# One expert-weight stream per block: second blocks of an expert moved behind all first blocks

## The reference, cut to what matters

```
logits = hf @ router_w + router_b                    # 256 tokens x 32 experts
top_val, top_idx = lax.top_k(logits, TOP_K)          # TOP_K = 4
top_w = softmax(top_val)
...                                                  # tokens are grouped by expert
def expert_block(xb, e):
    g = xb @ w_gate[e] + b_gate[e]                   # 1024 x 1024
    u = xb @ w_up[e] + b_up[e]                       # 1024 x 1024
    g = minimum(g, 7); u = clip(u, -7, 7)
    act = g * sigmoid(1.702 * g) * (u + 1)
    return act @ w_down[e] + b_down[e]               # 1024 x 1024
y[token] += row_weight * expert_block(...)           # summed over a token's 4 experts
```

## Time and profile before

| | us |
|---|---|
| median of three runs | 2422.86 |
| the profiled execution | 2423.9 |
| its span, first to last instruction | 2422.1 |
| PE busy | 2315.6 |
| DVE busy | 1048.4 |
| ACT busy | 691.4 |

### The profile page before, as it was taken

One profiled execution on the slowest core, in us unless ns is written; L12 is line 12 of the kernel. 1 busy time (PEld: TensorE's weight loads), 2 busy tenths in 40 slices (PEclk: granted clock), 3 DMA queues, 4 the chain that ended last, 5 costly groups with the idle time before them and its releaser, 6 DMA issues.

```text
span 2422.1 us, 34200 instructions
## 1 busy us (share of the span) xinstructions
PE 2315.6 (96%) x13529; PEld 1558.5 (64%) x13530; DVE 1048.4 (43%) x1491; ACT 691.4 (29%) x945; POOL 4.9 (0%) x6
## 2 busy tenths in 40 slices
PE   6999899999999999999997999979999999999999
PEld 4667733333333333333335999969989899999998
DVE  7665241111111111111115765556565655576654
ACT  2122221110101001111005353354443544454443
POOL 0000000000000000000000000000000000000000
PEclk8999999999999999999998999989999999999999
DMA  9366379979999999799996555535555245544552
GB/s 367 115 226 253 133 291 422 422 320 422 422 422 422 422 422 421 331 422 422 422 422 237 187 201 180 187 126 200 184 189 182 95 176 190 185 174 172 191 184 94
DMA packets 93888, 657.03 MB, mean 271 GB/s; under 512 B 10308, under 2 KB 13144, under 8 KB 14840
## 3 DMA queue, kind: packets, MB, share of 16 engines
q1 hardware_dynamic: 91104, 648.19, 67.9%
q10 hardware_dynamic: 2712, 7.82, 1.0%
HBM read 654.84 MB, written 1.13 MB: 271 GB/s over the span
## 4 chain that ended last, share of the span: by engine, by line
PE 78%; DMA 16%; DVE 2%; ACT 2%; issue 1%; SPq 1%; ACTq 0%; DVEq 0%
PE psum L841 14%; DMA ring<-in_w_exp 13%; PE psum L525 13%; PE psum L524 13%; PE psum L526 13%; PE psum L865 6%; PE psum L592 3%; PE psum L693 2%; PE psum L818 2%; PE psum L875 2%; PE psum L731 1%; DMA ring<-in_w_ada 1%; DVE arena L1683 1%; PE psum L855 1%; DMA ring<-in_w_ffn 1%
## 5 line engine op out<-in xcount | busy, mean ns | idle before, releaser
L427 DVE TENSOR_TENSOR ring_parts<-ring,ring_parts 128x2048 fp32r<-128x2048 f32 x181 | 414.2, 2291 | 302.3 <-ACT ring_parts L1446 297.6
L524 PE MATMUL psum<-x_parts,ring_parts 128*128 128x256 f32 x1920 | 540.0, 281 | 3.6 <-DVE arena_parts L1683 3.6
L525 PE MATMUL psum<-arena_parts,ring_parts 128*128 128x256 f32 x1920 | 541.7, 282 | 0.0
L526 PE MATMUL psum<-x_parts,ring_parts 128*128 128x256 f32 x1920 | 538.0, 280 | 0.0
L841 PE MATMUL psum<-ring,arena 128*64 128x512 f32 x2176 | 484.8, 596 | 22.5 <-DMA ring<-in_w_exp 22.5
L524 PEld LDWEIGHTS psum<-x_parts,ring_parts 128*128 128x128 f32 x1920 | 362.5, 189 | 7.0 <-issue 5.4
L1446 ACT ACTIVATE ring_parts<-ring 128x2048 fp32r<-128x2048 f32 x181 | 342.3, 1906 | 83.9 <-DMA ring<-in_w_mix 54.3
L526 PEld LDWEIGHTS psum<-x_parts,ring_parts 128*128 128x128 f32 x1920 | 363.3, 189 | 0.0
L525 PEld LDWEIGHTS psum<-arena_parts,ring_parts 128*128 128x128 f32 x1920 | 361.9, 188 | 1.7
L841 PEld LDWEIGHTS psum<-ring,arena 128*64 128x64 f32 x2176 | 154.3, 137 | 310.8 <-issue 310.8
L1680 DVE TENSOR_SCALAR arena<-psum 128x512 f32<-128x512 f32 x68 | 47.0, 692 | 626.7 <-ACT arena L1424 450.9
(11 more groups left out here) (270 smaller groups left out, 1944.6 us busy)
## 6 DMA issues: line engine op xcount, KB each, us to landing
ring<-in_w_exp SPq DMA_DIRECT2D x384, 1024.0 KB, 18.0
ring<-in_w_ffn SPq DMA_DIRECT2D x132, 1024.0 KB, 4.8
ring<-in_w_mix SPq DMA_DIRECT2D x49, 1024.0 KB, 4.8
ring<-in_w_ada SPq DMA_DIRECT2D x24, 1024.0 KB, 6.4
ring<-in_w_in SPq DMA_DIRECT2D x16, 1024.0 KB, 9.8
arena<-gain_scratch ACTq DMA_DIRECT2D x10, 512.0 KB, 3.5
ring<-in_w_out SPq DMA_DIRECT2D x4, 1024.0 KB, 4.8
ring<-in_w_attn SPq DMA_DIRECT2D x2, 1024.0 KB, 4.8
```

The costliest lines, as they stand in the source:

```text
L427: return engine.tensor_tensor(ring_parts[:, s, :], ring[:, s, :], ring_parts[:, RAW + s, :], ALU.subtract)
L524: mm(out, w[0], a[0], start=start, stop=False, **more)
L525: mm(out, w[0], a[1], start=False, stop=False, **more)
L526: return mm(out, w[1], a[0], start=False, stop=stop, **more)
```

## The change

SP no longer follows the block list by expert. It fetches the experts 1 to 31 for the blocks 1 to 31, one block each, and then, if there are more than 32 blocks, fetches for every further block all 12 pieces of its expert, taken from `etab`. The block list becomes: first block of expert 0, of expert 1, ..., of expert 31, and then the second and later blocks of those experts that have them. `extra` now counts only the blocks beyond the first. Since block b always has its own 12 arrivals, PE waits by the block's number b, and its register load of `etab` in each turn of the loop goes. The tables are made on 16 x 32 elements in place of 49 x 32, by more instructions, and `starts` and the first of the two `tables` signals are gone.

```diff
@@ block.sync @@
-            sp.wait_ge(sem("tables"), 1)
-            with sp.Fori(1, E) as e:
-                first = sp.value_load(starts[0:1, bass.ds(e, 1)], min_val=1, max_val=BLOCKS)
-                for n in range(EXPERT_PIECES):
-
-                    sp.wait_ge(pieces, first * EXPERT_PIECES + (N_PRE + n + 1 - EXPERT_PIECES))
-                    sp.dma_start(ring[:, n, :], row("w_exp", e * EXPERT_PIECES + EXPERT_ORDER[n])).then_inc(full[n], 16)
-
-            sp.wait_ge(sem("tables"), 2)
+            with sp.Fori(1, E) as e:
+                for n in range(EXPERT_PIECES):
+
+                    sp.wait_ge(pieces, e * EXPERT_PIECES + (N_PRE + n + 1 - EXPERT_PIECES))
+                    sp.dma_start(ring[:, n, :], row("w_exp", e * EXPERT_PIECES + EXPERT_ORDER[n])).then_inc(full[n], 16)
+
+            sp.wait_ge(sem("tables"), 1)
             blocks = sp.value_load(nblk[0:1, 0:1], min_val=E, max_val=E + EXTRA)
+            with sp.If(blocks > E):
+                with sp.Fori(E, blocks) as b:
+                    e = sp.value_load(etab[0:1, bass.ds(b, 1)], min_val=0, max_val=E - 1)
+                    for n in range(EXPERT_PIECES):
+                        sp.wait_ge(pieces, b * EXPERT_PIECES + (N_PRE + n + 1 - EXPERT_PIECES))
+                        sp.dma_start(ring[:, n, :], row("w_exp", e * EXPERT_PIECES + EXPERT_ORDER[n])).then_inc(full[n], 16)
@@ block.tensor @@
-            def expert_weights(n, expert):
-                pe.wait_ge(full[n], expert * 16 + 16 * (fills_before[n] + 1))
+            def expert_weights(n, b):
+                pe.wait_ge(full[n], b * 16 + 16 * (fills_before[n] + 1))
...
-            pe.wait_ge(sem("tables"), 2)
+            pe.wait_ge(sem("tables"), 1)
             blocks = pe.value_load(nblk[0:1, 0:1], min_val=E, max_val=E + EXTRA)
             with pe.Fori(1, blocks) as b:
-                expert = pe.value_load(etab[0:1, bass.ds(b, 1)], min_val=0, max_val=E - 1)
...
-                hidden(0, expert)
-                hidden(1, expert)
+                hidden(0, b)
+                hidden(1, b)
...
-                down(b, expert)
+                down(b)
@@ DVE, the tables @@
-            step(ts(extra, cnt, float(CAP), 1.0, ALU.is_gt, ALU.add))
+            step(ts(extra, cnt, float(CAP), None, ALU.is_gt))
...
-            v.tensor_copy(starts[:], start).then_inc(sem("tables"), 1)
-            step(tt(ended, across(co("block"), E), along(end_, BLOCKS), ALU.is_ge))
-            step(v.tensor_reduce(owner, ended, AX_X, ALU.add))
-            step(tt(ended, ended, along(extra, BLOCKS), ALU.mult))
-            step(v.tensor_reduce(ahead, ended, AX_X, ALU.add))
-            step(tt(ahead, co("block"), ahead, ALU.subtract))
-            ts(basetab[:], ahead, float(CAP), None, ALU.mult)
-            ts(etab[:], owner, float(E - 1), None, ALU.min)
-            ts(nblk[:], end_[:, E - 1:E], 0.0, None, ALU.add).then_inc(sem("tables"), 1)
+            step(tt(cmp_a, across(co("extra"), E), along(start, EXTRA), ALU.is_ge))
+            step(tt(cmp_b, across(co("extra"), E), along(end_, EXTRA), ALU.is_lt))
+            step(tt(picked, cmp_a, cmp_b, ALU.mult))
+            step(tt(cmp_a, picked, along(co("expert"), EXTRA), ALU.mult))
+            step(v.tensor_reduce(xe, cmp_a, AX_X, ALU.add))
+            step(tt(cmp_b, across(co("extra"), E), along(start, EXTRA), ALU.subtract))
+            step(ts(cmp_b, cmp_b, 1.0, float(CAP), ALU.add, ALU.mult))
+            step(tt(cmp_b, cmp_b, picked, ALU.mult))
+            step(v.tensor_reduce(xb, cmp_b, AX_X, ALU.add))
+            v.memset(etab[:], 0)
+            step(v.memset(basetab[:], 0.0))
+            v.tensor_copy(etab[:, 0:E], co("expert"))
+            v.tensor_copy(etab[:, E:E + EXTRA], xe)
+            v.tensor_copy(basetab[:, E:E + EXTRA], xb)
+            ts(nblk[:], end_[:, E - 1:E], float(E), None, ALU.add).then_inc(sem("tables"), 1)
```

More of the change, by code:

```diff
@@ L83 @@
 for _name, _w in (("ident", P), ("ones", P), ("before", P), ("rotate", P), ("causal", P), ("flip", P),
-                  ("inv_freq", 1), ("eps", 1), ("slot", CAP), ("slot_of_row", 1), ("block", BLOCKS),
+                  ("inv_freq", 1), ("eps", 1), ("slot", CAP), ("slot_of_row", 1), ("extra", EXTRA), ("expert", E),
                   ("bucket", 2 * T - 1), ("one_hot", E), ("group_sum", 1)):
@@ L135, in constants @@
     put("slot_of_row", (i % CAP)[:, None])
-    put("block", np.tile(np.arange(BLOCKS), (P, 1)))
+    put("extra", np.tile(np.arange(EXTRA), (P, 1)))
+    put("expert", np.tile(np.arange(E), (P, 1)))
     b = t5_bucket(np.arange(-(T - 1), T))
@@ L283, in build @@
         basetab = sb("basetab", [P, BLOCKS])
-        starts = sb("starts", [P, E], I32)
         nblk = sb("nblk", [P, 1], I32)
@@ L374, in build @@
         cnt, extra, start, end_, exc = (view(16664 + n * E, E) for n in range(5))
-        owner = view(16824, BLOCKS)
-        ahead = view(16824 + BLOCKS, BLOCKS)
-        ended = view(13312, BLOCKS, E)
+        xe = view(16824, EXTRA)
+        xb = view(16824 + EXTRA, EXTRA)
+        cmp_a = view(13312, EXTRA, E)
+        cmp_b = view(13312 + EXTRA * E, EXTRA, E)
+        picked = view(13312 + 2 * EXTRA * E, EXTRA, E)
         ada_parts = (ada_sum[:], diagonal[:].rearrange("p a i -> p (a i)"))
@@ L827, in turn_gathered, with hidden @@
                 last.then_inc(sem("g_turned"), 1)
-            def expert_weights(n, expert):
-                pe.wait_ge(full[n], expert * 16 + 16 * (fills_before[n] + 1))
+            def expert_weights(n, b):
+                pe.wait_ge(full[n], b * 16 + 16 * (fills_before[n] + 1))
                 return ring[:, n, :]
-            def hidden(which, expert):
+            def hidden(which, b):
                 bank, at_ = 4 + which, 4 * which
@@ L837, in hidden @@
                 for n in range(2):
-                    w = [expert_weights(at_ + 2 * n + half, expert) for half in range(2)]
+                    w = [expert_weights(at_ + 2 * n + half, b) for half in range(2)]
                     for k in range(4):
@@ L855, in spread, with down @@
                 mm(psum[:, 4, :], picked_e[0:E, :], posw[0:E, :], start=True, stop=True).then_inc(sem("spread_done"), 1)
-            def down(b, expert):
+            def down(b):
                 pe.wait_ge(sem("act_t_ready"), b + 1)
                 for n in range(4):
-                    w = expert_weights(DOWN_AT + n, expert)
+                    w = expert_weights(DOWN_AT + n, b)
                     for k in range(2):
@@ L913, in _ @@
             spread(0)
-            down(0, 0)
-            pe.wait_ge(sem("tables"), 2)
+            down(0)
+            pe.wait_ge(sem("tables"), 1)
             blocks = pe.value_load(nblk[0:1, 0:1], min_val=E, max_val=E + EXTRA)
             with pe.Fori(1, blocks) as b:
-                expert = pe.value_load(etab[0:1, bass.ds(b, 1)], min_val=0, max_val=E - 1)
                 pe.wait_ge(sem("hg_ready"), b + 1)
@@ L1419, in _ @@
             load_gain(0)
-            act.wait_ge(sem("tables"), 2)
+            act.wait_ge(sem("tables"), 1)
             blocks = act.value_load(nblk[0:1, 0:1], min_val=E, max_val=E + EXTRA)
@@ L2016, in _ @@
             step(tt(start, end_, extra, ALU.subtract))
-            v.tensor_copy(starts[:], start).then_inc(sem("tables"), 1)
-            step(tt(ended, across(co("block"), E), along(end_, BLOCKS), ALU.is_ge))
-            step(v.tensor_reduce(owner, ended, AX_X, ALU.add))
-            step(tt(ended, ended, along(extra, BLOCKS), ALU.mult))
-            step(v.tensor_reduce(ahead, ended, AX_X, ALU.add))
-            step(tt(ahead, co("block"), ahead, ALU.subtract))
-            ts(basetab[:], ahead, float(CAP), None, ALU.mult)
-            ts(etab[:], owner, float(E - 1), None, ALU.min)
-            ts(nblk[:], end_[:, E - 1:E], 0.0, None, ALU.add).then_inc(sem("tables"), 1)
-            dve.wait_ge(sem("tables"), 2)
+            step(tt(cmp_a, across(co("extra"), E), along(start, EXTRA), ALU.is_ge))
[13 more added lines that the diff above has]
+            ts(nblk[:], end_[:, E - 1:E], float(E), None, ALU.add).then_inc(sem("tables"), 1)
+            dve.wait_ge(sem("tables"), 1)
             dve.wait_ge(sem("line_read"), 2)
```

## The result

The changed kernel takes 2465.02 us (median of 4 runs, 2461.59 to 2470.54) against 2423.38 us before (4 runs beside it, 2419.94 to 2424.93). The ratio is 1.0169 with a 95% interval of 1.0154 to 1.0183: slower by 41.6 us. I had forecast 2454.5 us, 31 us slower, with 2450 to 2459 as the range. The direction was right, the time 10.5 us too short, outside the range.

A forecast was written before the change was run, and what follows sets the result against it. The prediction took the experts' stage as bound by weight transfers at 422 GB/s: 59.6 us of extra loads less 28.2 us of pauses gives +31.4 us on the profiled 2423.9, so a median of 2454.5 us, range 2450 to 2459.

The forecast's parts named there:

- The reading of the stage: Experts' stage: transfers at a 422 GB/s ceiling set the end, 29.8 us a block against PE's 27.6 us.
- The size of the stage: Experts' stage: 59.6 us of added loads less 28.2 us of vanished pauses, +31.4 us in sum.
- two pauses that are gone: Experts' stage: the stream's stops at the two second blocks, 14.8 and 13.4 us, disappear, together 28.2 us.
- The step that failed: After the last wait for an expert's piece, through the four layers: same instructions in the same order, no cost.
- The small edits at zero: Start of stream, SP's loop change, DVE's tables and PE's register load: each bounded by a few us, taken as 0.
- the wait for `starts`: Start of the expert stream: SP no longer waits for this table; gain between 0 and 7.6 us, taken as 0.
- The seam: Between SP's two load loops: a loop end, table loads and a branch, at most 2 us, taken as 0.
- The whole price of 59.6 us: Rival, experts' stage: the pauses were not lost time, so all 24 loads are paid, 2482.5 us; 3%.
- The slower stream: Rival, experts' stage: the two refetched sets run below full rate, at 320 GB/s giving 2473 us; 1%.
- a faster stream: Rival, experts' stage: an unbroken stream beats 422 GB/s, break-even at 436, at best 2398 us; 1% break-even, 1% better.
- missing reloads: Rival, experts' stage: the two second blocks do not exist at run time, time stays at 2423; 1%.

The follow-up runs named there:

- `in_place`: The kernel before, block order by expert kept, but every block fetches its own 12 pieces and PE waits by block: 2455.55 us, ratio 1.0131.
- `tiny_refetch`: The changed kernel with each of the 24 refetched pieces bringing only 128 of 2048 columns: 2458.37 us, ratio 1.0147 to the kernel before.
- `keep_starts`: The changed kernel with the removed tensor `starts` put back, unused: 2455.08 us.
- `after_pad256`: The changed kernel with 256 unused bytes per partition ahead of the arena: 2463.14 us, ratio 1.0171 to the kernel before.
- `after_pad64`: The changed kernel with 64 unused bytes per partition ahead of the arena: 2457.3 us, ratio 1.0143 to the kernel before.
- `before_x_too`: The kernel before with 128 unused bytes ahead of x and 128 more ahead of the arena: 2431.68 us, ratio 1.0037.
- `before_x_pad`: The kernel before with 128 unused bytes ahead of x alone, which also moves the arena: 2430.44 us, ratio 1.0036.

## Why the prediction was right and where it failed

**The reading of the stage was right.** The stream at 422 GB/s set the end, a set of pieces took 29.82 us for 26 periods in a row, no slice of the stage after the first products is below 422, and the waits of PE for pieces grew to 50 us where I had said some 55. The first wait came in block 6, where I had said that the lead would be used up in about six blocks and the waits be there from about the eighth. `in_place` shows that the bytes count and not the order, `tiny_refetch` that the reload is not priced by its bytes alone.

**The size of the stage was a little off.** +31.4 was forecast; measured were +32.5 in `keep_starts`, +33.4 in the second run of the changed kernel and +34.9 in the first. The terms stand, 24 pieces at 2.485 us and two pauses that are gone. What I left out is that the stream can also stop at its start. In the first profile it stood idle for 1.9 of 3 us (the window at 342 to 345 us above, 156 of 422 GB/s). PE ran at half clock just before, and its product down of block 0 took 8.88 us in place of 7.02. The granted clock over that stretch was 0.52 (PE busy, PEclk, DMA share, GB/s):

```profile
336.00:343.00 7.00, 7.00 (x17) 0.52 0.94 394
```

This is the lower of the clock's two levels, 1.2 GHz in place of 2.4, for most of the window. In the trace of the kernel before the same products ran at full clock and the stream had no such gap. But the half clock is not shown to be the cause. The second run of the changed kernel had the product down at 7.02 us and full clock, and a gap of about 1.5 us all the same (8 us at 341 of 422 GB/s; `after_pad256` shows 328):

```profile
342.00:350.00 8.00, 8.00 (x37) 2.54 (x35) 0.00 (x0) 0.60 (x1) 0.00 (x0) 1.00 0.92 341
```

Nor does a gap lengthen the stretch by its own size: `after_pad256` with it and `after_pad64` without it (419 GB/s in that window) both take 983.4 us. So 1 to 3.5 us of the stretch stay without a cause.

**The step that failed** is "What follows the last wait, half an up product, one product down and the four layers, is the same instructions in the same order", from which I took no cost. The sentence is true and the conclusion false: the instructions are the same and their operands are not in the same place. The change removes `starts` from the list of tensors, and I priced that at nothing without naming it. Its price is 8 to 9 us, shown in both directions: put back, 2464.45 becomes 2455.08; put into the kernel before, 2421.99 becomes 2430.33. With the tensor kept, the measured 2455.1 us lies within a microsecond of the forecast 2454.5, and its interval of 1.0111 to 1.0145 holds it. That close a match is in part luck. In its profile the stage is 32.5 us longer than before and not 31.4, the layers 3.3 us longer (1154.0 against 1150.7, at the same placement), and the part ahead of the stage 4.1 us shorter (316.84 against 320.93); the last two, which I had at nothing, nearly cancel.

**The small edits at zero stood.** DVE's tables were ready at 319.0 us, 3.3 us after the stage's first product, where before they took until 325.0, 4.1 us after it; ACT's first work behind the tables still waited for PE, from the end of its previous work to 322.77 us. The single instruction took 0.69 us, not the 0.58 I had scaled by size. SP's first load left 3.8 us after the first hidden product both times (319.48 - 315.70 and the earlier trace rows), so the wait for `starts` was worth nothing. The seam does not show in the stream: the first load behind it was issued at 1232.2 us, the stream stayed at 422 GB/s, and the second loop's loads took 20.7 to 25.3 us to land, so that several pieces were on their way when SP reached it:

```profile
DMA to landing us min/median/max: 20.7/23.2/25.3
```

**The rivals.** The whole price of 59.6 us did not come: the pauses had indeed been lost time. The slower stream did not come either; the refetched sets moved 422 GB/s like the others. Both rivals about a faster stream and missing reloads fell with the rows above. The actual miss was in none of them. The Trainium skill, DMA: Bandwidth & Descriptors, Specifications, lists about 358 GB/s per core as memory's limit; by that the sum would have been +42, which happens to be the measured total, but the windows disagree with it at 422 GB/s, and the missing 8 us lie in layers where the stream is at 174. A total that fits is no evidence for a term.

## What to carry to other kernels

When PE and the transfers are close in pace (here 27.6 and 29.8 us a block), ask of every pause of the stream what PE gains by it, and of every block moved out of the stream's shadow what it will cost alone: a reuse that stalls the stream for 14 us is still cheaper than a block at the end for 28.
## What the runs showed of the hardware that I had not expected

The pace of PE's pairs of weight load and product depends on where the operands begin in SBUF, the core's on-chip memory. With the arena at 0 modulo 256 bytes the layers' weight loads had a median of 188 ns; at 128, the place of x and of the ring, 192 ns; at 192, 187 ns. The kernels took 2455.1, 2464.5 (and 2463.1 with 256 bytes more), and 2457.3 us. The layers took 1150.7 to 1154.0 us in the three profiles with the arena and x as before, 1158.9 to 1163.1 in the six with the arena at the place of x or of the ring (`tiny_refetch` left out, its last stretch begins earlier), and 1156.6 with the arena at 192. The products over 512 columns behave the other way round: 395 ns with their two operands 128 bytes apart modulo 256, 390 with them at equal places. Which accesses collide, or whether any do, is not settled. Two theories about the short products failed on `before_x_too` and `before_x_pad`, which were slower by 10 and 9 us with the weight loads' median at 189 and 188 ns: their loss does not show in that number, though it does in the mean durations of the short products above. Not tried: moving the ring, and the distances of 32 and 96 bytes.
